# A trunk layer on one core: where the output gate's latent projection stands on TensorE

## The reference, cut to what matters

```python
(r, k, v, lw_f, lw_b, la_f, la_b, lg, q_g, k_g, v_g, og, lgk_f, lgk_b) = split_cols(h @ p['w_in'], IN_SPLITS)
...
rkv = short_conv(jnp.concatenate([r, k, v], axis=-1), p['rw_conv'], grid)      # 3x3 taps on latent tokens
g = jax.nn.sigmoid(lg) @ p['rw_g2']                                            # the output gate, low rank 128
kk = heads(k * p['rw_k_k'])
kk = kk * lax.rsqrt(jnp.sum(kk * kk, axis=-1, keepdims=True) + EPS)            # k's norm
...
bonus = (jnp.sum(rh * kh * p['rw_r_k'], axis=-1, keepdims=True) * vh).reshape(B, T, RW_W)
return (yn + bonus) * g, jnp.stack(finals, axis=1)
```

## Time and profile before

| | us |
|---|---|
| median of 3 runs | 939.52 |
| lowest and highest of them | 935.55, 941.69 |
| the profiled execution, timed as the runs are | 942.03 |
| its span, first to last instruction on the core | 939.4 |
| its mean granted TensorE clock | 0.968 of full speed |

### The profile page before, as it was taken

The page is one execution under the profiler, slowest core; times in us unless marked ns, Lnnn a source line. Parts: engine busy times, 40 slices in busy tenths (PEclk is TensorE's granted clock), DMA queues, the critical chain, the costliest instruction groups (busy, mean ns, idle before and its releaser), DMA issues.

```text
span 939.4 us, 21447 instructions
## 1 busy us (share of the span) xinstructions
PE 851.6 (91%) x8858; PEld 520.8 (55%) x8858; DVE 565.9 (60%) x940; ACT 331.4 (35%) x582; POOL 155.0 (17%) x302
## 2 busy tenths in 40 slices
PE   2899999999999979888887898899995999999995
PEld 0555455556555535677776777745663544444542
DVE  2523046699988799565565665697355344444467
ACT  3230111142034666366566663311310222222213
POOL 7000111113000104333222231010002000000051
PEclk9899999999899999899999999999995999999998
DMA  8923223224154201211211222591153899999956
GB/s 324 327 104 103 91 90 102 90 91 133 26 197 160 90 0 29 40 18 33 42 36 34 47 37 54 185 360 65 46 202 129 281 359 370 365 361 369 314 137 224
DMA packets 121007, 142.54 MB, mean 152 GB/s; under 512 B 50092, under 2 KB 86472, under 8 KB 120520
## 3 DMA queue, kind: packets, MB, share of 16 engines
q1 hardware_dynamic: 112072, 116.65, 37.8%
q0 software_dynamic: 3744, 13.63, 4.7%
q10 hardware_dynamic: 5088, 10.82, 3.0%
HBM read 123.08 MB, written 18.00 MB: 150 GB/s over the span
## 4 chain that ended last, share of the span: by engine, by line
PE 78%; DVE 11%; issue 4%; DMA 3%; ACT 3%; SPq 0%; ACTq 0%; DVEq 0%; POOLq 0%
PE bank L2037 71%; PE bank L2041 7%; DMA region<-in_w_ada_dram 3%; DVE rk_r L1451 2%; ACT region L969 1%; DVE region L1451 1%; DVE rk_r L1452 1%; DVE cl_b L1359 1%; DVE cl_b L1956 1%; DVE region L2026 1%; ACT ada_row_buffers L969 1%; DMA rk_r<-h_rows_dram,slot_tokens 0%; DVE region L2022 0%; DVE region L2005 0%; DVE region L1641 0%
## 5 line engine op out<-in xcount | busy, mean ns | idle before, releaser
L2037 PE MATMUL bank<-region 64*64 64x64 f32 (+3 forms) x3900 | 399.0, 298 | 14.3 <-issue 4.8
L2037 PEld LDWEIGHTS bank<-region 64*64 64x64 f32 (+1 forms) x3900 | 231.8, 148 | 169.3 <-issue 159.2
L969 ACT ACTIVATE region<-bank 128x256 f32<-128x256 f32 (+3 forms) x215 | 97.4, 453 | 342.7 <-PE bank L2037 255.1
L2037 PE MATMUL bank<-region,rk_r 128*128 128x512 f32 x176 | 80.2, 610 | 0.8 <-issue 0.8
L2041 PE MATMUL bank<-ident,region 128*128 128x128 f32 (+2 forms) x403 | 61.9, 282 | 12.9 <-DMA region<-in_c_dram 11.1
L2041 PEld LDWEIGHTS bank<-ident,region 128*128 128x128 f32 (+2 forms) x403 | 44.2, 142 | 31.5 <-issue 24.2
L2004 DVE TENSOR_SCALAR region<-region 128x256 f32<-128x256 f32 x16 | 4.7, 294 | 93.6 <-ACT region L969 93.6
L1451 DVE SCALAR_TENSOR_TENSOR rk_r<-region,vec,rk_r 128x512 f32<-128x512 f32 x64 | 50.1, 783 | 12.6 <-ACT rk_r L969 10.5
L2037 PEld LDWEIGHTS bank<-region,rk_r 128*128 128x128 f32 x176 | 33.7, 196 | 39.7 <-issue 38.5
L944 POOL DMA_INDIRECT rk_r<-h_rows_dram,slot_tokens x16 | 16.0, 998 | 227.2 <-PE bank L2041 127.5
L1633 DVE TENSOR_TENSOR region<-bank,region 128x256 f32<-128x256 f32 x60 | 25.5, 425 | 40.5 <-PE bank L2037 39.2
(11 more groups left out here) (283 smaller groups left out, 1135.9 us busy)
## 6 DMA issues: line engine op xcount, KB each, us to landing
region<-in_moe_w_dram SPq DMA_DIRECT2D x38, 1024.0 KB, 10.0
region<-in_w_ada_dram SPq DMA_DIRECT2D x12, 2048.0 KB, 8.5
region<-in_w_in_dram SPq DMA_DIRECT2D x6, 2048.0 KB, 8.4
cl_b<-in_moe_w_dram SPq DMA_DIRECT2D x10, 1024.0 KB, 10.5
expert_rows_dram<-yg_b ACTq DMA_DIRECT2D x14, 512.0 KB, 6.9
region<-late_condition_dram SPq DMA_DIRECT2D x3, 1024.0 KB, 9.2
a_rows_dram<-region SPq DMA_DIRECT2D x20, 128.0 KB, 2.8
region<-inverse_rows_dram SPq DMA_DIRECT2D x20, 128.0 KB, 3.1
```

The lines of the kernel that those rows point to most:

```text
L969: return act.activation(out, in_, func, **kw)
L2037: return pe.matmul(out, lhsT, rhs, start=start, stop=stop)
```

## The change

The gate's projection is cut in three. Its 8 latent products are taken out of `project("lg")` behind the bonus. The first five stand now before the norm products (kl, kc), the other three behind them; the bank of ("pl", "lg") stays open meanwhile, with the norm products going to other banks. The wait for the gate's weights moves with them. The counter `filled` is raised behind the fifth product, so that the job order holds, and a semaphore of its own, `s_lgl`, tells ACT when the sum is complete. ACT copies the latent gate inputs out right behind the exponential of the norms, before `conv_input("v1")`. Only the 8 context products stay behind the bonus, with their copy. In the job list ("pl", "lg") moves from behind the bonus to before ("kl", 0); thus every job from ("kl", 0) to the bonus gets the next bank, and jobs from ("pc", "lg") on have the bank that they had.

```diff
--- before.py
+++ after.py
@@ -346,9 +346,9 @@
             return [(key + "l", d, i) for i in range(RC)] + [(key + "c", d)]
         jobs += unit("k0") + [("ada", 8)] + unit("k1") + turn(8) + [("ada", 9)] + rank_jobs("w", 0)
         jobs += unit("k2") + turn(9) + [("ada", 10)] + rank_jobs("a", 0) + unit("k3") + turn(10) + [("ada", 11)] + rank_jobs("w", 1)
-        jobs += unit("v0") + turn(11) + rank_jobs("a", 1) + [("kl", i) for i in range(RC)] + [("kc",)]
+        jobs += unit("v0") + turn(11) + rank_jobs("a", 1) + [("pl", "lg")] + [("kl", i) for i in range(RC)] + [("kc",)]
         jobs += unit("v1") + [("L", 0, 0), ("L", 0, 1)] + unit("v2") + [("L", 1, 0), ("L", 1, 1)] + unit("v3")
-        jobs += [("bonus",)] + unit("lg")
+        jobs += [("bonus",), ("pc", "lg")]
         jobs += [("vt", t) for t in range(NT)]
         NS = 2 * NT
 
@@ -511,6 +511,7 @@
         LAST.update({"qk": ("pc", "g1"), "vg": ("vg", NT - 1), "og": ("og", NT - 1), "r": ("pc", f"r{RC - 1}"),
                      "k": ("pc", f"k{RC - 1}"), "v": ("pc", f"v{RC - 1}"), "lora": ("pc", "la")})
         s_wlg = sem("gate_weights_in")
+        s_lgl = sem("latent_gate_inputs")
         s_condt = sem("condition_columns")
         s_lgk = sem("gla_gate_weights")
         s_rawz = sem("conv_borders_zero")
@@ -1233,6 +1234,8 @@
                 out_of(A(sq[:, i, P:T], bank(("kl", i))[:, :], ACT.Ln, bias=eps6), "kl", i)
             out_of(A(sq[:, :, 0:P], bank(("kc",))[:, :].rearrange("p (c t) -> p c t", c=RC), ACT.Ln, bias=eps6), "kc")
             tell(A(sq, sq, ACT.Exp, scale=-0.5), s_kkn)
+            act.wait_ge(s_lgl, 1)
+            out_of(A(slg[:, P:T], bank(("pl", "lg"))[:, :]), "pl", "lg")
             conv_input("v1")
             decays(0)
             growths_for_b(0)
@@ -1246,7 +1249,7 @@
             raw_blocks(1)
             conv_input("v3")
             growths_for_k(0)
-            projected(slg, "lg")
+            copy_out(slg[:, 0:P], ("pc", "lg"), bank(("pc", "lg"))[:, 0:P])
             for t in range(NT):
                 copy_out(vtok[:, t], ("vt", t))
             for H in range(-1, NS):
@@ -2130,9 +2133,11 @@
             ada_turn(2)
             ada_turn(3)
 
-            def project(name, w, at=None, width=P):
-
-                for kind, sl in (("pl", slice(P, T)), ("pc", slice(0, P))):
+            LATENT, CONTEXT = ("pl", slice(P, T)), ("pc", slice(0, P))
+
+            def project(name, w, at=None, width=P, parts=(LATENT, CONTEXT)):
+
+                for kind, sl in parts:
                     b = open_bank(kind, name)
                     n = sl.stop - sl.start
                     for k in range(KT):
@@ -2558,6 +2563,14 @@
             project("v0", w, 0)
             ada_turn(11)
             low_rank("a", 1)
+
+            def gate_inputs(ks):
+                for k in ks:
+                    ins = mm(lgl[:, :], w_lg[k], hT[:, k, P:T], start=k == 0, stop=k == KT - 1)
+                return ins
+            pe.wait_ge(s_wlg, 32)
+            lgl = open_bank("pl", "lg")
+            finish(gate_inputs(range(0, 5)))
             for i in range(RC):
                 pe.wait_ge(s_prod, i + 1)
                 finish(mm(open_bank("kl", i)[:, :], blk[:, :], sq[:, i, P:T]))
@@ -2565,6 +2578,7 @@
             for i in range(RC):
                 ins = mm(b[:, i * P:(i + 1) * P], blk[:, :], sq[:, i, 0:P])
             finish(ins)
+            gate_inputs(range(5, KT)).then_inc(s_lgl, 1)
             project("v1", w, P)
             scores("L", 0)
             project("v2", w, 2 * P)
@@ -2576,8 +2590,7 @@
                 for i in range(RC):
                     ins = mm(b[:, t * NH + 2 * i:t * NH + 2 * i + 2], prod[:, i, t * P:(t + 1) * P], blk[:, 0:P:HD])
             finish(ins)
-            pe.wait_ge(s_wlg, 32)
-            project("lg", w_lg)
+            project("lg", w_lg, parts=(CONTEXT,))
             pe.wait_ge(s_conv, 3 * RC)
             for t in range(NT):
                 b = open_bank("vt", t)
```

## The result

| | us |
|---|---|
| changed kernel, median of 20 runs | 931.89 |
| before, median of 20 runs (the 3 of above among them) | 936.51 |
| ratio, 95% interval | 0.9950 (0.9935 to 0.9964) |
| the profiled execution of the changed kernel, its span | 932.11, 929.6 |

The change makes the kernel 0.5% faster, 4.6 us. One of the 20 runs of the changed kernel took 1741.74 us and is left out of the ratio; without it the median would be 931.67. The forecast was 936.2 us, a gain of 3.3 us or 0.35%, with a range from 932.5.

A forecast was written before the change was run, and what follows sets the result against it. PE bounds the start of the vt transposes, 7.57 us behind DVE; 7.6 less a 1.7 us push of DVE gives 5.8, so 942.03 - 5.8 = 936.2 us, 3.3 below the median 939.52. Range 932.5 to 940.5.

The forecast's parts named there:

- Step 1: Norm products: PE's idle time falls from 3.94 to about 0.8 us at full clock; kc ends 0.65 us earlier.
- Step 2: Behind kc: v1 ends 1.9 us later, block scores start 1.7 us later; the new ACT copy is hidden under v1.
- Step 3: In front of vt: DVE's last convolution replaces PE as bound; vt starts at about 384.2, not 390.01, gaining 5.8 us.
- Step 4: From vt's first transpose to the loop's first scores: 4.28 us unchanged, and the 5.8 us carried to the end.
- How the profiled run stands to the median: Profiled 942.03 us lies 2.5 above the plain median, likely unlucky half clock; so 936.2, gain 3.3 us against the median.
- Rival B: Typical runs of before lack the half clock in this stretch, so gain 1.1 us, time 938.4; chance 0.2.
- D: Clock falls ahead of kl, scores 5.3 us late; loses 2.3 against before without half clock, 941.8; chance 0.05.
- C: Half clock from vt into the loop: +1.6 us at transposes, 1.6 in the loop; gain 2.6, 939.4; chance 0.15.

The follow-up runs named there:

- one_of_eight: The kernel before with only one of the gate's eight latent products, the other seven left out and nothing put ahead of v1; ratio 0.9928 to before.
- all_behind_kc: All eight latent products in one piece between the norm products and v1, the same PE work taken from behind the bonus; ratio 1.0016 to before.
- change_one_context: The changed kernel with only one of the gate's eight context products behind the bonus, the other seven left out; ratio 0.9958 to before.
- again_before: The kernel before once more, nothing edited, for a second profile and the spread; ratio 0.9995 to before, profiled span 935.5 us.
- change_filled_gap: The changed kernel with four extra products behind v1, filling the gap ahead of the block scores, nothing moved; ratio 0.9957 to before.

## Why the prediction was right or wrong

**Step 1, the norm products: right.** The gap is 0.75 us (0.8 forecast), the clock there is 1.00, ACT's logarithms start 10.0 us after the first product, not 10.4, so 0.4 earlier where I had 0.65.

**Step 2, v1 and the block scores: right.** The scores come 2.0, 1.6 and 1.7 later in the three profiles; 1.7 was forecast. The added copy is hidden under v1.

**Step 3, the bound changes hands: right in kind, and shown; its size was 1.2 us too large.** The transposes start with the end of the last convolution in all three profiles. one_of_eight, all_behind_kc and change_one_context show it from three sides. The size was off in one term: I had DVE shifted by the same 1.7 and then wrote that a bound by DVE doesn't see PE's clock. It does. `conv("v2")` and `conv("v3")` wait for taps from PE's v2 and v3, and with 6.7 us of half clock behind the scores' gap the last convolution ended at 55.7, where 53.8 was forecast; with 3.4 us it ended at 53.9. At the loop's scores the gain was 3.8, 5.6 and 5.1 us, and 5.8 was the sum; the medians have 4.6.

**Step 4, behind it: right on the whole.** 4.3 us from transposes to scores, in two of three profiles; 4.8 in the third, at half clock. The gain was not lost in the loop.

**How the profiled run stands to the median: wrong, and this is the step that failed.** The forecast of 936.2 is the profiled 942.03 less the sum, 5.8, set against the median of three runs. I took the 2.5 us by which the profiled execution lay over that median off the gain, as if they had been the stretch's own half clock, which the change would remove. again_before, a run of 938.26 us and within 0.5 us of the median beside it, has the same 64.0 us in the stretch and the same granted clock of 0.89. The excess of the profiled execution over it lay elsewhere, 1.5 us ahead of the stretch and 2.5 behind it, so there was nothing to take off. Rival B rested on the same thought, and both profiles of before speak against it.

**The level.** The same step took its median from three runs, and 939.52 lies 3.0 us above the 936.51 of the 20. The error of 4.3 us in the time is thus 3.0 of level, plus 2.5 taken off the gain without ground, less the 1.2 by which the sum of 5.8 was too large. In the gain alone, 3.3 is 1.3 below the 4.6, and 5.8 would have been 1.2 above it. That the forecast gain came as near as it did is luck: a deduction without ground made up for a sum that was too large. The range went on its lower side from the lowest run less the too small gain. With 5.8 in its place that bound would have been 935.55 - 5.8 = 929.8, and 931.89 inside.

**Slips in the numbers.** None of these moves the forecast. 935.55 - 3.3 is 932.25, not 932.5; the result lies below both. The latent products' "10.0 less the overlap" are 8.58 + 1.02 = 9.6 less the overlap, which gives the 9.4 that the sum of that step names. The kernel before without any half clock has its first transpose at 384.4 in rival B and at 385.2 in D.

**Rivals.** B fell: its gain of 1.1 us is a ratio of 0.9988, outside the interval. C was not what the change does, but change_one_context shows it at its price: +1.4 us up to the loop, where I had +1.6. The second 1.6, inside the loop, no run separates. The rule that I had weighed it by, in the Trainium skill, TensorE: Matmul & The Clock Gate, Part 4 (PE-mode transpose), that transposes don't count for the clock, is not settled by these runs. change_one_context agrees with it: 20 transposes ran from 381.56 on for 4.53 us, all at half clock, and the clock came up only at 390.6. change_filled_gap speaks against it: there PE idled 1.92 us, then had only transposes from 378.71 on, and the clock came up at 381.4 in their midst; but context products stood ahead of the idle time, and what brought the clock up is not isolated. D did not occur: the clock stayed up over the short gap in all seven profiles that have it.

## What to carry to other kernels

Work that is moved into one engine's idle time pays only for what that engine was last for, and costs what it delays behind it; so look at the moved work's successors first. Here the same eight products were worth 0% with all of them in one piece ahead of v1 and the idle time left as it was, 0.5% with five in the first idle time and three ahead of v1, and 1.1% with those three behind v1, in the second; 2.6 us of the last are not explained by their place. Before a profiled execution is corrected to a median, find the place of its excess: compare where the same landmark lies in two profiles of the same kernel. And three runs are few for the base of a forecast: here their median was 3.0 us high, as much as the gain that was forecast.

## What the runs showed of the hardware that was not expected

- In change_filled_gap a gap filled with products of no use had the clock up behind it (1.00 from 350.5 to 369.3), but the clock then fell behind the bonus and stayed down for 6.8 us, into the transposes. Mean clock (0.974) and time (0.9957) were those of the change.
- The 40 two-column products of the bonus keep PE busy without a gap for 4.5 to 6.3 us, and in all 15 profiles the clock falls under them or within 1 us behind them, as it does at an idle gap of 4 us.
- Half clock on PE also delays an engine that waits for it: DVE's last convolution ended 28.1 to 28.2, 29.2 to 29.4 and 30.8 us behind the block scores' start with 0, 3.4 and 6.8 us of half clock behind the gap.
- Taking work away from PE ahead of a wait can cost: with seven narrow products less, the gap was 3.82 us and the clock stayed at 1.2 GHz for 13.7 us.
- One kernel's runs lie up to 14 us apart (931.93 to 945.6 for before, in 109 runs), and go with the mean granted clock by 7.5 us for 0.01, at a correlation of -0.70.
